# Two post-norm layers on one Trainium2 core: the first input weights in half chunks, and identity products ahead of and between the real ones

## What is computed

```python
# layer 0: one projection D -> [u 512 | q 512 | k 512 | v 512]
hcat = x @ w_in
u, q, k, v = jnp.split(hcat, [512, 1024, 1536], axis=-1)
mix = jnp.concatenate([pool_mixer(u), stick_breaking(q, k, v)], axis=-1) @ w_out
# layer 1: RWKV-7 mixer; its first product takes the keys of the token-shifted input
xk = x + xx * mu[2]
k = xk @ w_k
# both layers: 64 SwiGLU experts of width 256, top 8 of 64 by a sigmoid router, and one shared expert
ff = routed_experts(x) + swiglu(x, ws_gate, ws_up, ws_down)
```

## Time and profile before

| | before |
|---|---|
| median of 3 runs | 1392.91 us (1391.98 to 1393.37) |
| the profiled execution, its own time | 1387.37 us |
| its span, first to last instruction | 1385.6 us |
| PE busy | 1344.1 us, 97% of the span |
| DVE, ACT, POOL busy | 436.5, 271.4, 93.9 us |
| read from HBM | 448.26 MB, 324 GB/s over the span |
| mean granted clock of PE | 0.992 of full speed |

### The profile page before, as it was taken

One profiled execution on the slowest core, in us unless ns is written; L12 is line 12 of the kernel. 1 busy time (PEld: TensorE's weight loads), 2 busy tenths in 40 slices (PEclk: granted clock), 3 DMA queues, 4 the chain that ended last, 5 costly groups with the idle time before them and its releaser, 6 DMA issues.

```text
span 1385.6 us, 24728 instructions
## 1 busy us (share of the span) xinstructions
PE 1344.1 (97%) x10364; PEld 779.2 (56%) x10364; DVE 436.5 (32%) x982; ACT 271.4 (20%) x533; POOL 93.9 (7%) x124
## 2 busy tenths in 40 slices
PE   7999999999999999979999998999999999999997
PEld 6889443444434444339688998944444443434433
DVE  2245122222222222146652337622222222222213
ACT  1231211111111111112421331121111111111111
POOL 7202000000000000012003100300000000000001
PEclk9999999999999999999999999999999999999999
DMA  4697799999999999975323006679999999999993
GB/s 152 178 358 310 305 364 408 422 422 422 421 422 422 422 422 422 421 251 171 115 101 124 4 4 245 258 292 374 398 422 422 422 422 422 422 422 421 422 420 156
DMA packets 98666, 450.45 MB, mean 325 GB/s; under 512 B 16032, under 2 KB 45344, under 8 KB 48928
## 3 DMA queue, kind: packets, MB, share of 16 engines
q1 hardware_dynamic: 98592, 449.34, 80.9%
HBM read 448.26 MB, written 1.05 MB: 324 GB/s over the span
## 4 chain that ended last, share of the span: by engine, by line
PE 93%; DVE 5%; issue 1%; DMA 1%; ACT 1%; POOL 0%; SPq 0%; DVEq 0%; PEldq 0%; ACTq 0%
PE PS L1882 31%; PE PS L1921 17%; PE PS L1929 10%; PE PS L1853 7%; PE PS L549 4%; PE PS L512 3%; PE PS L1396 2%; PE PS L1373 2%; PE PS L1358 2%; PE PS L1901 1%; PE PS L1521 1%; PE PS L2002 1%; PE PS L1536 1%; PE PS L1545 1%; PE PS L1893 1%; PE PS L534 1%
## 5 line engine op out<-in xcount | busy, mean ns | idle before, releaser
L2234 DVE TENSOR_TENSOR y_parts<-PS,y_parts 128x512 fp32r<-128x512 f32 x128 | 88.5, 691 | 216.7 <-ACT y_parts L2136 216.7
L2208 DVE SCALAR_TENSOR_TENSOR AR<-AR,PS 128x256 f32<-128x256 f32 x64 | 30.8, 481 | 386.5 <-ACT AR L2114 386.5
L1929 PE MATMUL PS<-y_parts,token_map 128*128 128x512 f32 x496 | 146.6, 417 | 0.0
L1882 PE MATMUL PS<-AR,xT 128*64 128x512 f32 x512 | 115.7, 593 | 5.6 <-issue 5.5
L1929 PEld LDWEIGHTS PS<-y_parts,token_map 128*128 128x128 f32 x496 | 83.5, 188 | 60.9 <-issue 50.3
L1921 PE MATMUL PS<-AR 128*64 128x512 f32 x512 | 116.9, 598 | 0.0
L1921 PE MATMUL PS<-RING,AR 128*64 128x512 f32 x496 | 116.9, 598 | 0.0
L1882 PE MATMUL PS<-AR 128*64 128x512 f32 x512 | 115.5, 592 | 0.0
L2136 ACT CAST y_parts<-PS 128x512 fp32r<-128x512 f32 x128 | 75.0, 586 | 172.0 <-PE PS L1921 172.0
L1882 PE MATMUL PS<-RING,xT 128*64 128x512 f32 x480 | 108.1, 592 | 0.0
L1882 PE MATMUL PS<-RING,AR 128*64 128x512 f32 x480 | 108.1, 592 | 0.0
(11 more groups left out here) (315 smaller groups left out, 1575.7 us busy)
## 6 DMA issues: line engine op xcount, KB each, us to landing
RING<-in_moe_w_gate SPq DMA_DIRECT2D x64, 1024.0 KB, 11.8
RING<-in_moe_w_up SPq DMA_DIRECT2D x64, 1024.0 KB, 13.9
AR<-in_moe_w_gate SPq DMA_DIRECT2D x64, 1024.0 KB, 13.2
AR<-in_moe_w_up SPq DMA_DIRECT2D x64, 1024.0 KB, 15.2
AR<-in_moe_w_down SPq DMA_DIRECT2D x64, 1024.0 KB, 14.0
RING<-in_moe_w_down SPq DMA_DIRECT2D x62, 1024.0 KB, 15.1
AR<-in_ab_w_in SPq DMA_DIRECT2D x8, 1024.0 KB, 5.6
AR<-in_rw_w_o SPq DMA_DIRECT2D x4, 1024.0 KB, 5.3
```

The costliest lines, as they stand in the source:

```text
L1882: ins = nc.tensor.matmul(PS[s * B:(s + 1) * B, 4, :], gathered(k)[:, c:c + B], gate_and_up(slots[s])[:, k, :, :], start=(k == 0), stop=(k ...
L1929: ins = nc.tensor.matmul(PS[:, 2 * t + h, :], OHT[:, half, t, :], YS[:, n, h * 512:(h + 1) * 512], start=False, stop=True, skip_group_chec ...
L2208: nc.vector.scalar_tensor_tensor(out=HH[0:2 * B, :].rearrange("p (k j) -> p k j", k=FT), in0=by_row(SIL[0:2 * B, :]), scalar=GC[:, buf:buf ...
L2234: nc.vector.tensor_tensor(YS[:, 1, h * 512:(h + 1) * 512], PS[:, 5 + h, :], YS[:, 0, h * 512:(h + 1) * 512], ALU.subtract).then_inc(q["low ...
```

## The change

There are three parts, and a few edits that move no work.

1. `load_chunk` issues two transfers where it issued one: input rows k 0 to 3 of a chunk, and k 4 to 7, 512 KB each, with a semaphore for each half (`s_wl` and the new `s_wr`). `project_channels` waits for the first half ahead of a chunk, and for the second ahead of the product k = 4 of its first tile. `project_tokens` and the output projection wait for both halves where they waited for one transfer.
2. `busy(bank, count)` is new: PE multiplies the identity by itself `count` times, into a bank that nothing reads. Six such products stand ahead of the first transposes, two behind them (both in bank 0), and ten behind the transposes of layer 1's first tokens (bank 6).
3. The semaphores `keys_scaled` and `count_ready` go; what waited for them waits for the step count of DVE and for `rank_ready`, which is counted up at the same place. An unused function and unused parameters go as well.

```diff
         def load_chunk(sp, src, b, c):
-            sp.dma_start(chunk(b), src[:, :, ds(c * CB, CB)]).then_inc(s_wl[b], 16)
+            for half, loaded in enumerate((s_wl[b], s_wr[b])):
+                ks = slice(4 * half, 4 * half + 4)
+                sp.dma_start(chunk(b)[:, ks, :], src[:, ks, ds(c * CB, CB)]).then_inc(loaded, 16)
...
@@ project_channels
                         for k in range(KT):
-                            if k == KT // 2 and b == 0 and c == 0 and x_whole:
-                                x_whole()
+                            if k == KT // 2 and c == 0:
+                                pe.wait_ge(s_wr[b], 16 * i + 16 * (base // 2 + 1))
                             ins = nc.tensor.matmul(PS[:, 4 + 2 * b + c, 0:T], chunk(b)[:, k, c * P:(c + 1) * P],
                                                    x[:, k, :], start=(k == 0), stop=(k == KT - 1))
...
@@ project_tokens
-                    pe.wait_ge(s_wl[b], 16 * i + 16 * (base // 2 + 1))
+                    for loaded in (s_wl[b], s_wr[b]):
+                        pe.wait_ge(loaded, 16 * i + 16 * (base // 2 + 1))
...
+        def busy(bank, count):
+
+            for n in range(count):
+                nc.tensor.matmul(PS[:, bank, (n % 4) * P:(n % 4) * P + P], ident[:, :], ident[:, :], start=True, stop=True)
+
         def pe_mix0(pe):
+            pe.wait_ge(s_const, 1)
+            busy(0, 6)
             pe_transpose(pe, 0, 0)
             pe_transpose(pe, 0, 1)
+            busy(0, 2)
             pe.wait_ge(s_xT, 4)
             project_channels(pe, xT, 0, 6, 0)
...
                     pe.wait_ge(s_wl[c - 2], 16 * 5)
+                    pe.wait_ge(s_wr[c - 2], 16 * 5)
...
@@ dve_mix1
-            ins.then_inc(r["keys_scaled"], 1)
+            link(ins)
...
-            v.wait_ge(r["keys_scaled"], 1)
+            link.sync()
...
@@ pe_mix1
             pe_transpose(pe, 2, 0)
+            busy(6, 10)
             pe.wait_ge(s_vec, 16 * 12)
...
@@ the expert parts of SP, PE and ACT
-                sp.wait_ge(q["count_ready"], 1 + past["count_ready"])
+                sp.wait_ge(q["rank_ready"], 1 + past["rank_ready"])
```

More of the change, by code:

```diff
@@ L316, in program @@
         s_wl = [sem(f"mixer_chunk_loaded{b}") for b in range(2)]
+        s_wr = [sem(f"mixer_chunk_rest_loaded{b}") for b in range(2)]
         s_wo = [sem(f"mixer0_out{c}_loaded") for c in range(2, 4)]
@@ L481, in swapped, with project_channels @@
             return x.rearrange("p (t a r) -> p t a r", t=TT, a=2)[:, :, ::-1, :]
-        def project_heads(pe, x, base, chunks, tile0, x_whole=None):
+        def project_channels(pe, x, base, chunks, tile0):
             with pe.Fori(0, chunks // 2) as i:
@@ L828, in program @@
         s_lhc = sem("lora_hidden_ready")
-        names = ["input_turned", "first_keys", "head_maps_ready", "keys_scaled", "head_squares_done",
+        names = ["input_turned", "first_keys", "head_maps_ready", "head_squares_done",
                  "head_squares_guarded", "root_ready", "norm_ready", "norm_spread", "log_decay_ready", "key_norm_used",
@@ L1734, in pe_core @@
             project_out(pe, KTT, WO, 1, loaded, last_chunk=lambda: pe_transpose(pe, 3, 0))
-        once = ["logits_done", "scores_ready", "mask_ready", "rank_done", "rank_ready", "count_ready",
+        once = ["logits_done", "scores_ready", "mask_ready", "rank_done", "rank_ready",
                 "first_gates", "shared_gate", "shared_gate_up", "shared_silu", "shared_hidden", "gates_split", "pads_cleared"]
@@ L2050, in pe_moe @@
                     pe_pair(pe, PAIRS - 4 + p, p, OCTS - 1, False, last=(p == 3))
-                pe.wait_ge(q["count_ready"], 1 + past["count_ready"])
+                pe.wait_ge(q["rank_ready"], 1 + past["rank_ready"])
                 most = nc.tensor.value_load(cnti[0:1, 2 * l:2 * l + 1], min_val=0, max_val=T)
@@ L2168, in act_moe @@
                     act_pair(s, PAIRS - 4 + p, p, OCTS - 1, False, last=(p == 3))
-                s.wait_ge(q["count_ready"], 1 + past["count_ready"])
+                s.wait_ge(q["rank_ready"], 1 + past["rank_ready"])
                 most = nc.scalar.value_load(cnti[0:1, 2 * l:2 * l + 1], min_val=0, max_val=T)
@@ L2297, in dve_route @@
                 v.sem_inc(q["rank_ready"], 1)
-                v.sem_inc(q["count_ready"], 1)
                 onehot(0, 8, q["onehot_ready"], q["slots_ready"])
```

## The result

The changed kernel takes 1378.47 us (median of 4 executions, 1377.25 to 1381.24), the kernel before 1392.45 (4 executions, 1388.9 to 1393.37): ratio 0.9907, 95% interval 0.9884 to 0.9930, so about 13 us (9.7 to 16.2) of 1392. In a second comparison, six executions of the changed kernel on another chip, it was 1379.48 against 1390.91: 0.9919 (0.9896 to 0.9943), 11.4 us between the medians. The forecast of 1389.4 was wrong, and so was its range, which ended at 1387.1.

What follows compares the result with a forecast made beforehand. PE, holding 93% of the chain, was taken as the bound. The start's -3.56 and zeros elsewhere, rounded to -3.5, came off the median of 1392.91 us for a forecast of 1389.4, range 1387.1 to 1392.2.

Steps and rivals of the forecast that it cites:

- Waits and semaphores: PE's program and the ends of DVE and the expert loop: one more wait per chunk, two removed, worth 0.
- The start: First products of `w_in`: begin at 8.6 instead of 10.98 and end at 50.78 instead of 54.34, 3.56 us sooner.
- The clock: Stretch of 96 `w_in` products: 1.96 us of its 43.36 went to half clock and would be gained.
- The early start: Chunk 0 of `w_in`: four products run early, worth 1.73 us, less 0.12 for the later second half.
- Will the clock be held?: Before the `w_in` products: identity products leave PE idle 0 to 1.5 us before 8.6, likely keeping full clock.
- Rival B: Start of `w_in`: PE begins at 8.6 but at half clock as long as before; gain 2.4 us, 1390.5; chance 0.17.
- The middle products: Ten identity products between the layers: fill idle time, clock falls all the same, 0; bound -2.26 if held.
- rival E: Clock held both at the start and between the layers: -3.5 - 2.26, 1387.1 us; chance 0.06.
- The other chunks: Later chunk loads in halves: extra issues are covered by slack, so 0.
- Rival D: Chunk stream falls behind PE: 6.6 us lost, less the 3.5 gained, 1396.0 us; chance 0.06.
- C: Chunk 0's halves both land at 10.9, or late rounds' weight stream swallows the gain: 1392.9 us; chance 0.19.
- The second half at 12.9: Chunk 0's second half, with a fixed cost of about 2 us per transfer paid in series: gain of 1.8.

## Why the prediction was wrong

**The step that failed** is the term for PE's own program, "Waits and semaphores ... **0**", together with the costing of the added products by what they do on the array. An instruction also has a place in PE's program. I read the 2.01 us ahead of line 1936, used it as an example of a gap that loses the clock, and took it as given, though its releaser was only "issue". It was PE's own code coming late, and the change moved that code. Removing the branch is worth 6.8 us on the kernel before and nothing on the changed one: 6.8 of the 11.4 us that separated the two on that chip. The sum had nothing for it. The parts of it that the profiles of before and after show are 1.86 for the stop and 1.70 for the half clock behind it; the second branch, which was in time in both profiled executions and late in three of the others, is the likely rest. There it took 3.4 to 3.9 us, and from the branch to the last work of the kernel it was 13.1 to 14.4 us where it was late, and 10.6 where it was in time: 2.5 to 3.7 us. Whether it is late in most executions of the kernel before isn't shown, since only one is profiled.

**The start was right in kind and a little small.** Forecast 3.56, in the profiles 4.33. The clock was priced a little high: the half clock cost 1.64 us (43.36 - 41.72), and not 1.96, since a tile at full clock takes 3.48 us (41.72 / 12) and not the 3.45 read from ACT's copies. The early start was priced low, at 1.73 - 0.12. The second half of chunk 0 was not 0.12 later than the old whole transfer but about 1.3 sooner, at 9.6, so PE never broke off behind the fourth product, and the whole earlier begin counts, 10.98 - 8.29 = 2.69. And PE began at 8.29, below the 8.5 that I had as the bound, since the identity products had let the transposes run faster: the bound held only without them. Work of this kind alone gives 3.5 to 4.1 us without the branch. So forecast and start agree. That the two parts need each other fits, but the runs can't settle it: 1.1 and 0.0 us apart by the medians, or 2.4 and 0.6 by the ratios, against 4.1 together, with an interval of some 2.5 us each way on each ratio.

**Will the clock be held?** Yes, over a gap of 0.65 us. The eight products aren't needed for it every time: with two columns it held too, over 0.63 us, and with half chunks alone over 1.01. With them it had risen before the gap in nine of nine profiled executions, without them in five of eleven. The prediction held a gap of 2.01 or 3.10 us for one that loses the clock, and that isn't sure either: with start products alone it held over 3.04 us in one execution (stretch 41.72) and fell over 3.55 in another. Rival B, and with it the rule of the Trainium skill, TensorE: Matmul & The Clock Gate, Part 4, that transposes don't let full clock engage, did not come about: in the kernel with two-column products little but transposes ran before 9.05, the last transpose took 273 ns behind others of 421, and the stretch of 96 products took 41.72, all at full clock.

**The middle products**: 0 by work, as forecast; the clock fell at 617.2, so rival E didn't come about. By their length they move the packet ahead of the second branch from 4.4 to 11.5 us; that this is worth up to 3 us in some executions is likely and not shown. The price for a held clock, up to 2.26, was too high: 26 products gave 1.1 at the place and nothing in the total.

**The other chunks**: 0, right; halves land 3.4 to 5.4 us after issue. Rival D is refuted, and C with it: nothing was swallowed, since PE reached the rounds of the first expert loop 4.2 to 4.3 us sooner (186.07 against 190.38, 539.86 against 544.06). The second half at 12.9, by the rule that the prediction took from the Trainium skill (DMA: Bandwidth & Descriptors, section Bandwidth), didn't come about: it landed at 9.6, since the halves overlapped. That page gives the fixed cost in its section Anatomy of one DMA, for transfers that GpSimd issues, and here SyncE issued them.

**The comparison itself.** I took a shift from one profiled execution over to a median that lay 5.5 us above it and didn't ask what these 5.5 were. Part of them is what the change removed: taking the branch out took 6.8 us off the median, 3.2 more than the 3.56 that the profile showed. The rest stays open.

## What to carry to other kernels

A stop of an engine that has no releaser ("issue") right behind a branch, above all one that jumps over code that never runs, may be the engine's own code arriving late: look at the branch's own duration and at the instruction queue, and price it as something that any added or removed instruction ahead of it can take away or bring. Before crediting an edit, give the kernel the same number of instructions without the work (two-column products do) and compare over a dozen executions. When the profiled execution lies well below the median, something in the other executions costs that much, and a forecast for the median has to name it.

## What the runs showed of the hardware

- Instructions came in 16 KB packets (61 of them, 1.00 MB, in the kernel before). PE's branch over unused code took 0.33 to 0.47 us when the last packet had started at least 3.4 us ahead of it, and 2.35 to 3.85 us when one started from 0.2 us ahead to 1.1 us behind its start; it then ended 2.4 to 2.8 us after the packet's start.
- Where it was late in the first layer, it was so by placement: with 32 more instructions ahead still late, with 36 not, in the profiled executions. The packet moved from 0.2 to 8.6 us ahead of the branch between the two. Why the second layer's branch is late in one execution and in time in another with the same number of instructions (32 more) stays open.
- A late branch can cost twice: the stop, and 1.70 us in the next eight products when the clock falls (5.37 against 3.67 us).
- At the start, the clock was held over idle gaps of 0.63, 0.65 and 1.01 us, and once over 3.04 us; it fell over gaps of 3.10 and 3.55 us. Between the layers it fell behind ten two-column products and a gap of 4.48 us, as it did behind ten whole ones and 4.39 us. In the kernels without whole products at the start it rose during the last transposes in five of eleven executions (273 ns behind others of 417 to 421), and in the other six it hadn't risen when they were done.
- Two halves of 512 KB, issued 0.5 us apart, landed 6.5 and 7.4 us after issue, the second at 9.6, where the transfer of 1024 KB landed at 10.86 in the kernel before and between 9.9 and 11.6 in the others that load it whole.
